# Moving three PSUM evacuations ahead of the weight conversions, and a column sum into the attention loop, in a fused two-block transformer kernel

## The reference

```python
ada = jax.nn.silu(c) @ w_ada[l] + b_ada[l]          # six vectors: shift, scale, gate for mixer and FFN
h = rms_norm(x, g_pre_mix[l]) * (1.0 + scale_m) + shift_m
z = h @ w_in[l]
c_q, c_kv, k_rope, q_g, k_g, v_g, a_g, r_g = split_cols(z, IN_SPLITS)
# mla_mixer, 8 heads:
q = (rms_norm(c_q, g_q) @ w_uq).reshape(B, S, H, MLA_QK_DIM)
k_nope = (c_kv @ w_uk); v = (c_kv @ w_uv)           # c_kv normalised before
q_rope, k_rope = apply_rope(...)
p = softmax(where(causal, q @ k.T, NEG_INF)); o = p @ v
o = jnp.concatenate([o_mla, o_gla], axis=-1) @ w_out[l]
x = x + gate_m * rms_norm(o, g_post_mix[l])
```

## Time and profile before

| | |
|---|---|
| median of three runs | 2858.18 us (2851.34 to 2860.84) |
| the profiled execution | 2851.34 us, of which 2849.6 us are the span from the first to the last instruction |
| mean granted TensorE clock | 0.964 of full speed |
| PE busy | 2676.9 us (94%) |
| PEld busy | 2203.6 us (77%) |
| DVE busy | 1660.1 us (58%) |
| ACT busy | 1155.2 us (41%) |

### The profile page before, as it was taken

The page is one execution under the profiler, slowest core; times in us unless marked ns, Lnnn a source line. Parts: engine busy times, 40 slices in busy tenths (PEclk is TensorE's granted clock), DMA queues, the critical chain, the costliest instruction groups (busy, mean ns, idle before and its releaser), DMA issues.

```text
span 2849.6 us, 31255 instructions
## 1 busy us (share of the span) xinstructions
PE 2676.9 (94%) x12332; PEld 2203.6 (77%) x12332; DVE 1660.1 (58%) x1682; ACT 1155.2 (41%) x1207; POOL 0.2 (0%) x4
## 2 busy tenths in 40 slices
PE   5899989789999999997999999899789999999997
PEld 4678768678888888886987777778667888888886
DVE  7778577656665555556345566554554555555556
ACT  4234534433333333334334444434553333333333
POOL 0000000000000000000000000000000000000000
PEclk8899989899999999998999999999999999999999
DMA  8979757957775555553744444355345555555553
GB/s 315 335 267 324 256 207 285 256 177 255 250 247 203 187 189 191 191 191 97 226 159 130 143 138 145 133 181 192 115 137 188 186 183 191 191 191 188 187 188 129
DMA packets 267760, 566.00 MB, mean 199 GB/s; under 512 B 9711, under 2 KB 46477, under 8 KB 258590
## 3 DMA queue, kind: packets, MB, share of 16 engines
q1 hardware_dynamic: 265614, 561.72, 58.4%
q10 hardware_dynamic: 2064, 3.15, 1.0%
HBM read 559.59 MB, written 5.24 MB: 198 GB/s over the span
## 4 chain that ended last, share of the span: by engine, by line
PE 79%; DVE 9%; ACT 4%; issue 4%; DMA 2%; SPq 1%; DVEq 0%; ACTq 0%
PE bank L1152 24%; PE bank L1154 23%; PE bank L1153 23%; ACT wh L595 3%; DVE wl L1822 2%; DVE ACC L1992 2%; DVE ROWB L1822 1%; PE bank L1123 1%; PE bank L1640 1%; DMA raw<-in_w_xkv 1%; DVE X L1945 1%; PE bank L1692 1%; DMA raw<-in_w_in 1%; SPq L434 1%; DVE ACC L1843 1%
## 5 line engine op out<-in xcount | busy, mean ns | idle before, releaser
L1822 DVE TENSOR_TENSOR wl<-raw,wh 128x2048 fp32r<-128x2048 f32 (+4 forms) x434 | 975.4, 2248 | 897.5 <-ACT wh L595 896.9
L595 ACT ACTIVATE wh<-raw 128x2048 fp32r<-128x2048 f32 (+4 forms) x434 | 816.2, 1881 | 1270.3 <-PE bank L1154 1187.0
L1152 PE MATMUL bank<-wh,XTh 128*128 128x512 f32 (+4 forms) x2680 | 1050.8, 392 | 36.9 <-DVE wl L1822 31.8
L1153 PE MATMUL bank<-wl,XTh 128*128 128x512 f32 (+4 forms) x2680 | 1038.1, 387 | 0.0
L1154 PE MATMUL bank<-wh,XTl 128*128 128x512 f32 (+4 forms) x2680 | 1037.9, 387 | 0.0
L1152 PEld LDWEIGHTS bank<-wh,XTh 128*128 128x128 f32 x2680 | 509.5, 190 | 142.2 <-DVE wl L1822 26.2
L1154 PEld LDWEIGHTS bank<-wh,XTl 128*128 128x128 f32 x2680 | 508.9, 190 | 95.5
L1153 PEld LDWEIGHTS bank<-wl,XTh 128*128 128x128 f32 x2680 | 509.6, 190 | 91.7 <-issue 0.2
L1152 PE MATMUL bank<-wh,HTh 128*128 128x512 f32 x704 | 277.7, 394 | 9.5 <-DVE HTl L1822 3.6
L1154 PE MATMUL bank<-wh,HTl 128*128 128x512 f32 x704 | 275.2, 391 | 0.0
L1153 PE MATMUL bank<-wl,HTh 128*128 128x512 f32 x704 | 275.2, 391 | 0.0
(11 more groups left out here) (300 smaller groups left out, 1468.5 us busy)
## 6 DMA issues: line engine op xcount, KB each, us to landing
raw<-in_w_ada SPq DMA_DIRECT2D x96, 1024.0 KB, 6.0
raw<-in_w_in SPq DMA_DIRECT2D x48, 1024.0 KB, 5.2
raw<-in_w_ffn_gate SPq DMA_DIRECT2D x44, 1024.0 KB, 5.2
raw<-in_w_ffn_up SPq DMA_DIRECT2D x44, 1024.0 KB, 5.2
raw<-in_w_ffn_down SPq DMA_DIRECT2D x44, 1024.0 KB, 5.0
raw<-in_w_gate SPq DMA_DIRECT2D x44, 1024.0 KB, 5.1
raw<-in_w_up SPq DMA_DIRECT2D x44, 1024.0 KB, 5.2
raw<-in_w_down SPq DMA_DIRECT2D x44, 1024.0 KB, 5.1
```

The lines of the kernel that those rows point to most:

```text
L595: act.activation(wh[:, st.lin % 2, 0:width], raw[:, st.raw % 4, 0:width], ACT.Copy).then_inc(hi_made, 1)
L1152: pe.matmul(out_, hi_t[:, k, rows], w[0][:, q, :], start=first and q == 0, stop=False)
L1153: pe.matmul(out_, hi_t[:, k, rows], w[1][:, q, :], start=False, stop=False)
L1822: return dve.tensor_tensor(out_, a, b, op)
```

## The change

It has two parts. On ACT, the conversion `hi(uq1)` no longer stands ahead of the evacuation of chunk 0; the conversion of each next slab stands behind the evacuation of the chunk before, and one more conversion, `hi(uk)`, closes the sequence. On PE, `mod_sum(3)` is taken from behind the loop over the heads and put into its step 9, between the turn of head 7's probabilities and the value products of head 6.

```diff
             for c in range(3):
-                hi()
-                skip()
+                if c:
+                    hi()
+                    skip()
                 chunk_evac(CHUNK0["uq"] + c, lambda r: qrow[r][:, :, :].rearrange("p h d -> p (h d)")[:, 512 * c:512 * c + 512],
                            512, scale=QKD ** -0.5, done=45 + c)
+            hi()
+            skip()
...
+                if t == MH + 1:
+                    for _ in range(7):
+                        st.next(False)
+                    pe.wait_ge(S("masked"), MH)
+                    mod_sum(3)
                 h = t - 3
                 if 0 <= h < MH:
                     pe.wait_ge(S("pT_out"), h + 1)
...
-            for _ in range(7):
-                st.next(False)
-            pe.wait_ge(S("masked"), MH)
-            mod_sum(3)
```

## The result

| | before | after |
|---|---|---|
| median of 8 runs | 2855.95 us (2849.48 to 2860.84) | 2868.67 us (2863.97 to 2873.41) |
| ratio | | 1.0052, 95% interval 1.0036 to 1.0067 |
| the profiled execution | 2851.34 us, span 2849.6 | 2876.88 us, span 2875.1 |
| granted clock | 0.964 | 0.958 |

The kernel is slower by 0.52%, that is +14.9 us (10.3 to 19.1) by the ratio; the two medians lie 12.7 apart.

The account below looks back on a forecast made before the run. PE, 79% of the chain, was taken to bound the kernel; +14.5 us for the conversions and +3.3 for the column sum made +17.8, so 2858.18 became 2876.0 us, range 2863 to 2886.

Parts of the forecast that it names:

- both places: Query projection, where late conversions were to cost +14.5 us, and end of the heads, where the moved sum cost +3.3.
- the first term: Query projection: the late conversions cost +14.5 us, bounds 10.6 and 16.
- the second: End of the heads: the moved column sum costs +3.3 us, bounds +1.0 and +4.1.
- The closed chain: Query projection: evacuation, conversion, subtraction, then PE; 5.37 us of PE idle at each of three places, +10.6 us.
- The clock at the projection: Behind the new gaps PE runs at 1.2 GHz: chunk 1 +2.5 us, first kT bank +1.4.
- The column sum by its order: End of the heads: with equal clocks, head 7's value products end later and the turn of o starts +1.0 us later.
- The column sum by its clock: End of the heads: the moved sum runs mostly at 1.2 GHz, +2.3 us, three quarters of a possible +3.1.
- The prediction's own proof in the earlier trace: After an earlier column sum, PE was said busy 2.10 of 2.10 us with the clock at 0.50.
- the rival: Heads at another clock: high throughout, 2871.5 us in all, chance 0.14; or all slow, 2880.1, chance 0.13.
- Nothing later absorbs a delay.: Behind both places: each later stage waits for PE or for slabs at most four ahead, so the +17.8 us stays.

Follow-up runs that it names:

- e1: Kernel before with only the three conversions moved behind the evacuations, the column sum at its old place; ratio 1.0048 (1.0032 to 1.0064).
- e3: Kernel before with only the conversion of w_uk moved behind the evacuation of chunk 2; ratio 1.0018 (1.0006 to 1.0029).
- e4: Kernel before with the three conversions moved, plus 18 spare PE matmuls behind each of the three chunks; ratio 1.0043 (1.0028 to 1.0059).
- e5: Kernel before with the column sum moved, plus two spare float32 matmuls ahead of head 7's probability turn; ratio 1.0006 (0.9994 to 1.0018).
- e2: Kernel before with only the column sum moved into step 9 of the heads; ratio 1.0019 (1.0006 to 1.0031).
- e10: Kernel before plus 11 spare PE matmuls behind v, in the wait ahead of the heads; ratio 0.9991 (0.9980 to 1.0002).
- e8: Kernel before with the column sum moved ahead of head 7's probability turn; ratio 1.0017 (1.0006 to 1.0029).
- e6: Kernel before with DVE reordered at the projection: gate gain ahead of chunk 1's subtraction, gated output behind chunk 2's; ratio 0.9977 (0.9965 to 0.9990).
- e9: Kernel before with e6 and e10 together, plus the spare matmuls of e5, column sum at its old place; ratio 0.9970 (0.9957 to 0.9984).

## Why the prediction was right

The forecast was +17.8 and 2876.0 us, with a range of 2863 to 2886; measured were +14.9 by the ratio and 2868.67. The direction, both places and the mechanism held. Of the 7.3 us by which 2876.0 is too high, 2.2 are the median of before, which three executions put at 2858.18 and eight at 2855.95, and 5.1 are the change. In the profile the two places add up to 14.02 + 3.88 = 17.9, against 14.5 + 3.3 = 17.8; that they agree so well is partly luck, since the first term was too high and the second too low.

- **The closed chain.** 5.37 us of idle at each of three places was forecast and 5.39 is what each row shows, in after, e1 and e3 alike; e3 shows that each place counts by itself. The sum of the gaps, 16.2 - 5.5, is +10.7, forecast +10.6.
- **The clock at the projection.** +3.9 was forecast (2.5 at chunk 1, 1.4 at `kT`). The projection took 14.02 longer, forecast 14.5: 10.67 are the gaps, 2.18 chunk 1 (7.90 in place of 5.72), 1.31 the first `kT` bank (2.94 in place of 1.63), and -0.14 chunk 2. e4 shows the cause by holding the clock up. The forecast did not say that chunk 2, slow before, could get faster by it too; it does (-2.5).
- **The column sum by its order.** +1.0 was forecast, e5 measures +1.1.
- **The column sum by its clock.** +2.3 was taken between 0 and 3.1; after shows 3.88 for the whole second part and e2 4.2, so 2.8 to 3.1. This term was set too low; nearly all passes ran at 1.2 GHz. The Trainium skill, "TensorE: Matmul & The Clock Gate", section "Why this matters for your kernels", advises to keep TensorE busy and free of long idle gaps for the full clock. Steady work of this kind did not keep it: inside the sum of after PE is busy 4.00 of 4.00 us at 0.50. With the idle time filled the clock stayed up in e4, e10 and, until the sum was over, in e5, as the advice has it; e8, down behind gaps of 0.89 and 0.71, shows that there is more to it. The prediction's own proof in the earlier trace rows was weaker than it said: in the second window PE was busy 2.79 of 4.20 us, not all through, and the first is not behind a sum but over the end of one, and there it does show a busy PE at 0.50:

```profile
310.22 4.45 PE L1188 MATMUL bank<-CON,ACC 128*128 128x1 f32 x32
```

- **How firm the +3.9 is.** It compares with executions in which the sum ran fast at its old place. It did so in the profiles of before, e1, e3 and e6 (3.83 to 3.99), but not in e4 and e10 (6.83) and in part in e9 (4.60). So on average over executions the second part may cost less than 3.9; the ratio of e2, 2 to 9 us, allows both.
- **The heads.** They were left out of the sum, and the rival had them at another clock. They stayed as they were:

```profile
414.30 0.56 DVE L1826 TENSOR_TENSOR prob<-bank,CON 128x384 f32<-128x384 f32 x1 [0.96 <-PE bank L1459]
...
419.43 0.56 DVE L1826 TENSOR_TENSOR prob<-bank,CON 128x384 f32<-128x384 f32 x1 [1.67 <-PE bank L1459]
...
429.04 0.55 DVE L1826 TENSOR_TENSOR prob<-bank,CON 128x384 f32<-128x384 f32 x1
...
433.13 0.55 DVE L1826 TENSOR_TENSOR prob<-bank,CON 128x384 f32<-128x384 f32 x1
```

Heads 1 and 2 are 5.13 apart, 4 and 5 are 4.09, as in the earlier trace rows to 0.01 us. The heads as a whole took 0.75 less.

- **"Nothing later absorbs a delay."** That is nearly so for the waits. 0.37 us of the second part came back at once: DVE's `lo()` of the first `w_out` slab now starts at 454.19, ahead of the turn of `o`, and PE's next turns follow 2.84 behind the first ones in place of 3.21; first before, then after:

```profile
438.71 1.97 PE L1123 MATMUL bank<-CON,Z 128*128 128x128 f32 x8 [1.41 <-DVE XTl L1822]
```

```profile
457.13 1.97 PE L1126 MATMUL bank<-CON,Z 128*128 128x128 f32 x8 [0.90 <-DVE XTl L1826]
```

It is not so for the clock. The 25.5 us between the spans are 1.64 ahead of chunk 0's evacuation, 14.02 at the projection, -0.75 in the heads, 3.88 at their end, and 6.7 behind. The larger part of the last is in the 60 us from 100 us behind the turn of `o`, between mixer and FFN; first before, then after:

```profile
535.50:595.50 60.00, 35.48 (x165) 28.48 (x166) 34.79 (x53) 25.03 (x28) 0.00 (x0) 0.80 0.70 132
```

```profile
554.30:614.30 60.00, 36.19 (x148) 29.38 (x147) 31.33 (x51) 22.54 (x26) 0.00 (x0) 0.69 0.72 135
```

The mean clock there was 0.80 and 0.69, and the FFN's first `SIL` starts 166.5 instead of 160.3 behind the turn of `o`. The program is the same there. Of the eleven profiles only before and e8 take 160.3 and 160.4; e2 and e9 take 162.7 and 163.3, and all others 165.4 to 166.6, among them e5, e6 and e10, in which ACT's order at the projection is that of before. So this stage is not slow because of the late conversions. Why an execution gets one or the other was not settled; a shift of the work ahead of it may matter, chance may be all. These 6.2 us explain about half of the 12.8 by which the profiles are further apart than the medians. The forecast's +17.8 lies 5.1 above the difference of the medians, 12.7, and inside the ratio's interval; that this rest is luck of the clock and no term of the sum is argued, not shown.

## What to carry to other kernels

An instruction that prepares the next piece of work must not stand on its engine behind one that waits for the current piece: the preparation then comes out from under the main engine's work, with its whole chain, and once for every piece. A filler for idle time belongs ahead of the wait that makes the idle, and its duration is to be taken at the clock that it will meet there, not at the one of its old place; e8 had the place right and the duration wrong, and lost. Where an engine waits for a second one, look at what the second does first: in e6 a new order of the same instructions won 6.6 us of the whole kernel (3 to 10), where e10's filler, with a larger gain in its own place, won 2.6 (-1 to 6).

## What was not expected of the hardware

Whether the first heads run at 2.4 or 1.2 GHz is worth 6.3 us of 46.6, and both profiles with 2.65 us of spare matmuls in the idle time ahead of them (e10, e9) ran them at 2.4; of the nine without, only e3's did. In the other eight, heads 0 and 1 were masked 4.42 or 4.43 apart, also where PE's first turns of the stage still ran at 2.4 GHz (in after, the turn of the rotated key takes 0.41 for two passes, before 0.63). The heads' own work kept the high clock but did not bring it back for the first two or three heads. And a gain won at one place in this way was partly lost at the next: in e4 and e10 the column sum, at its old place, took the turn of `o` from 6.84 to 9.95 and 9.94.

A busy PE was not enough for the high clock here. PE worked without a gap all through the sums, and still the clock fell inside one (after, and 310 to 315 in before) or at its end (e5), and in e8 it did not come back during the 6.99 us of one. In before it did come back at the start of the sum at the end of the heads, behind twelve passes of value products (0.77 between 431.70 and 433.00, then 1.00). The same 32 passes take 3.8 us at 2.4 GHz and 6.8 to 7.0 at 1.2.
